# A decoder layer on one core: the half tiles of the output product in another order

## What is computed

```python
mix = gates[:, :, 0] * y_gla + gates[:, :, 1] * y_dsa
out = mix @ w_out[l]
x = x + gate_m * rmsnorm(out, g_post_mix[l])
h = rmsnorm(x, g_pre_ffn[l]) * (1.0 + scale_f) + shift_f
y = hier_moe(h, w_router_g[l], b_router_g[l], w_router_e[l], b_router_e[l], w_e_gate[l], w_e_up[l], w_e_down[l])
x = x + gate_f * rmsnorm(y, g_post_ffn[l])
```

## Time and profile before

| | |
|---|---|
| median of 3 runs | 761.08 us (760.99 to 763.07) |
| the profiled execution | 760.1 us, span of its records 758.3 us |
| TensorE busy | 684.6 us (90%) |
| VectorE busy | 410.4 us (54%) |
| ScalarE busy | 290.1 us (38%) |
| transfers | 179.27 MB, 236 GB/s over the span |

### The profile page before, as it was taken

How to read it: one execution, slowest core, us unless ns; L and a number is a source line. 1 busy time by engine, 2 the same in 40 slices (tenths; PEclk the granted TensorE clock), 3 DMA queues, 4 the chain that set the end, 5 groups by cost and what they waited for, 6 DMA issues and landing times.

```text
span 758.3 us, 9653 instructions
## 1 busy us (share of the span) xinstructions
PE 684.6 (90%) x3423; PEld 434.7 (57%) x3423; DVE 410.4 (54%) x867; ACT 290.1 (38%) x528; POOL 122.4 (16%) x156
## 2 busy tenths in 40 slices
PE   1899989998999989899999999989899978888785
PEld 0347757666777767778888888853333323333222
DVE  2376956998888886654523835645341211121127
ACT  5141435464486568643214233342121211121214
POOL 3056672320001011010000000040122111111100
PEclk9999989999999999999999999999989999999998
DMA  8989660411303030113334193999999999999973
GB/s 331 404 291 389 240 253 1 121 42 70 112 0 112 1 112 1 50 62 111 111 128 165 44 372 124 368 381 420 420 419 418 419 420 419 420 420 411 413 321 139
DMA packets 50319, 179.27 MB, mean 236 GB/s; under 512 B 9641, under 2 KB 13844, under 8 KB 36446
## 3 DMA queue, kind: packets, MB, share of 16 engines
q1 hardware_dynamic: 44502, 166.78, 56.2%
q0 software_dynamic: 4752, 8.18, 3.0%
q10 hardware_dynamic: 1016, 3.68, 1.3%
HBM read 174.13 MB, written 12.59 MB: 246 GB/s over the span
## 4 chain that ended last, share of the span: by engine, by line
PE 43%; DVE 22%; issue 7%; DMA 6%; SPq 5%; ACT 5%; DVEq 0%; POOL 0%; ACTq 0%; POOLq 0%
PE psA L498 8%; PE psA L500 7%; PE psA L499 7%; PE psS L916 6%; PE psA L945 5%; SPq L1130 4%; PE psG L916 4%; DVE mk_mem L1916 4%; DVE m L1915 3%; DMA arena<-in_w_e_up_dram 2%; DVE arena_r L1864 2%; DMA y_dram<-sig_mem,tables 2%; DVE mk_mem L1955 1%; DVE qs_mem L1935 1%; DVE qs_mem L2083 1%
## 5 line engine op out<-in xcount | busy, mean ns | idle before, releaser
L498 PE MATMUL psA<-arena_r 128*128 128x512 f32 x320 | 130.1, 406 | 0.0
L499 PE MATMUL psA<-arena_r 128*128 128x512 f32 x320 | 125.9, 393 | 0.0
L500 PE MATMUL psA<-arena_r 128*128 128x512 f32 x320 | 125.8, 393 | 0.0
L1864 DVE TENSOR_TENSOR arena_r<-arena,arena_r 128x1024 fp32r<-128x1024 f32 (+1 forms) x37 | 61.5, 1687 | 31.6 <-ACT arena_r L1377 30.5
L498 PEld LDWEIGHTS psA<-arena_r 128*128 128x128 f32 x320 | 60.9, 190 | 20.0 <-issue 8.1
L916 PE MATMUL psS<-arena,kv 128*64 128x512 f32 x224 | 59.9, 616 | 11.0 <-issue 9.3
L500 PEld LDWEIGHTS psA<-arena_r 128*128 128x128 f32 x320 | 60.8, 190 | 13.4
L499 PEld LDWEIGHTS psA<-arena_r 128*128 128x128 f32 x320 | 61.0, 191 | 12.1 <-issue 0.2
L916 PE MATMUL psG<-arena,kv 128*64 128x512 f32 x208 | 60.1, 630 | 6.3 <-issue 6.3
L1377 ACT CAST arena_r<-arena 128x1024 fp32r<-128x1024 f32 (+1 forms) x34 | 49.9, 1499 | 15.7 <-DMA arena<-in_w_in_dram 9.8
L2389 DVE TENSOR_TENSOR sig_mem<-sig_mem,psS 128x256 f32<-128x256 f32 x8 | 4.9, 611 | 77.0 <-ACT sig_mem L1710 77.0
(11 more groups left out here) (464 smaller groups left out, 1329.9 us busy)
## 6 DMA issues: line engine op xcount, KB each, us to landing
arena<-in_w_e_gate_dram SPq DMA_DIRECT2D x24, 1024.0 KB, 16.7
arena<-in_w_e_up_dram SPq DMA_DIRECT2D x24, 1024.0 KB, 19.7
arena<-in_w_in_dram SPq DMA_DIRECT2D x10, 2048.0 KB, 8.1
arena<-in_w_e_down_dram SPq DMA_DIRECT2D x12, 1024.0 KB, 19.2
qs_mem<-in_w_e_down_dram SPq DMA_DIRECT2D x10, 1024.0 KB, 23.4
arena<-in_w_ada_dram SPq DMA_DIRECT2D x4, 2048.0 KB, 16.6
qT<-in_w_ada_dram SPq DMA_DIRECT2D x6, 1024.0 KB, 5.0
gvs<-in_w_ada_dram SPq DMA_DIRECT2D x5, 1024.0 KB, 5.5
```

The source lines that it names most:

```text
L498: nc.tensor.matmul(acc, lhs[0], rhs[0], start=start, stop=False)
L499: nc.tensor.matmul(acc, lhs[0], rhs[1], start=False, stop=False)
L500: return nc.tensor.matmul(acc, lhs[1], rhs[0], start=False, stop=stop)
L1864: V.tensor_tensor(lo[:, part], src[:, part], hi[:, part], ALU.subtract).then_inc(lo_ready, 4 if q is None else 1)
```

## The change

The half tiles come in the order (0,0) (0,1) (1,0) **(2,0) (3,0) (1,1)** (2,1) (3,1). The work that hangs on tile 1 moves with (1,1): its turn goes into (2,1), its router into (3,1), its ranks behind router 2, its routing on VectorE behind `residual(2)`, its position behind `root_x1(2)`, its part of the first pair behind `residual(3)`, and its row store on ScalarE behind `out_root(2)`. The number and shapes of all instructions stay as they were.

```diff
-        out_order = [(0, 0), (0, 1), (1, 0), (1, 1), (2, 0), (3, 0), (2, 1), (3, 1)]
+        out_order = [(0, 0), (0, 1), (1, 0), (2, 0), (3, 0), (1, 1), (2, 1), (3, 1)]
...
             out_half(1, 0, turn=0)
-            out_half(1, 1, logits=0)
+            out_half(2, 0, logits=0)
+            out_half(3, 0)
             ranks(0)
-            out_half(2, 0, turn=1)
-            out_half(3, 0, logits=1)
+            out_half(1, 1)
+            out_half(2, 1, turn=1)
+            out_half(3, 1, turn=2, logits=1)
+            router(2)
             ranks(1)
-            out_half(2, 1)
-            out_half(3, 1, turn=2)
-            router(2)
             slots(0)
-            slots(1)
             first_rows(0, (0,))
             x1_turn(3, ("S0", "A0"))
             router(3)
+            slots(1)
             ranks(2)
...
             store_rows(0)
+            out_squares(2, 0)
+            out_squares(3, 0)
             out_squares(1, 1)
             out_root(1)
             x1_part(1)
-            out_squares(2, 0)
-            store_rows(1)
-            out_squares(3, 0)
             out_squares(2, 1)
             out_root(2)
+            store_rows(1)
             x1_part(2)
...
             out_scaled(1, 0)
+            out_scaled(2, 0)
             route(0)
+            out_scaled(3, 0)
+            position(0)
+            first_member(0)
             out_scaled(1, 1)
             residual(1)
-            position(0)
             turned(1)
             root_x1(1)
-            out_scaled(2, 0)
-            route(1)
-            out_scaled(3, 0)
-            position(1)
-            for tt in range(2):
-                first_member(tt)
-                first_slots(tt)
+            first_slots(0)
             out_scaled(2, 1)
             residual(2)
+            route(1)
             turned(2)
             root_x1(2)
+            position(1)
             out_scaled(3, 1)
             residual(3)
+            first_member(1)
+            first_slots(1)
             route(2)
```

## The result

| | before | changed |
|---|---|---|
| median of 4 runs, us | 761.04 (760.67 to 763.07) | 765.15 (764.33 to 766.25) |
| the profiled execution, its span, us | 760.1, 758.3 | 764.33, 762.5 |

The ratio is 1.0053, with a 95% interval of [1.0034, 1.0073]: slower, by 4.1 us. The forecast was 764.0.

The account below looks back on a forecast made before the run. The end was taken to hang on SyncE's weight-queue release, set by when VectorE begins route(2). +1.9 (wait) and +1.05 (moved work) gave +3.0 us: 763.1 profiled, 764.0 against the median; range 762.1, with some tenths, to 766.2.

Parts of the forecast that it names:

- the one number that decides: When VectorE begins route(2), now 490.06; the release of SyncE's weight queue and the first expert pair follow it; forecast +3.0 us.
- The loads' head start: SyncE's second-pair loads start 8.3 us earlier, near 466.4, but the queue then runs dry; costed at nothing.
- TensorE up to the end of (3,1): Same TensorE work in another order, ending 0.2 us earlier, with turns finding x1 ready; costed at nothing.
- the thin cover of `route(1)`: VectorE's route(1) and turned(2) end at 486.2, router 2 needs them at 486.24; cost nothing or a tenth.
- The wait of position(1): On VectorE, position(1) waits for ranks(1) behind router 2, so out_scaled(3,1) starts at 489.3 against 487.44: +1.9 us.
- The rival in which only the moved work counts: ranks(1) is there when VectorE reaches position(1), so no wait; +1.05 and up to 0.7 more, 762.1 to 762.8; chance 0.18.
- first_member(1) and first_slots(1): On VectorE they now stand between residual(3) and route(2), all on the path: +1.05 us.
- The clock, "so I add nothing": TensorE stops about 1.8 us ahead of the turn of tile 3; clock assumed to stay at 1.00, nothing added.
- the other end: If TensorE's clock falls to half at that stop, a further +2.8 us or so.
- The rival "the clock falls": TensorE's clock falls at the stop, or router 2 slips: +3.0 + 2.8, time 766.9; chance 0.10.
- The four loads: Sign that the forecast is right: SyncE issues the second pair's four loads near 466.4, now at 474.71.
- the wait ahead of line 2252: Sign that the forecast is right: VectorE idle there for tile 1 until ranks(1) releases it near 488.4.

Follow-up runs that it names:

- e1: The changed kernel with ranks(1) ahead of router 2 on TensorE; 762.75 us, ratio 1.0023.
- e2: The changed kernel with the second half of first_rows(0) and slots(1) moved ahead of the turn of tile 3 on TensorE; 763.34 us, ratio 1.0019.
- e5: The kernel before with only first_member(1) and first_slots(1) moved between residual(3) and route(2); 761.48 us, ratio 1.0004.
- e6: The kernel before with the third pair's second half of gate and up loads (2 MB) issued ahead of the wait for tile 3's rows; 761.81 us, ratio 0.9999.
- e9: The changed kernel with tile 1's position, first_member and first_slots behind route(2) on VectorE, and ranks(2) ahead of slots(1) on TensorE; 761.49 us, ratio 1.0004.
- e10: As e6 against the kernel before, but only one of the two 1 MB loads ahead of the wait; 762.91 us, ratio 1.0025.
- e11: As e7 against the kernel before, but only one of the two 1 MB loads ahead of the wait; 762.58 us, ratio 1.0020.
- e3: The changed kernel with SyncE waiting for (2,1) instead of (3,0) before the second pair's loads; 765.81 us, ratio 1.0049.
- e7: The kernel before with e6's earlier loads and router 1 inside (2,1) instead of (3,0); 761.06 us, ratio 0.9992.

## Why the prediction was right, and where it was off

*What bounds the kernel.* Held in part. Where the later places keep up, the end moves by as much as the release (e1 +1.7 and +1.6, e2 +3.0 and +2.9, e5 +1.0 and +1.0). But the release is not the one number that decides: the queue can run dry behind it, at the fourth pair's load (the change, 0.87 in 514 to 517) or at the fifth's (e6). In e6, e9, e10 and e11 the release moves by 0.0 to 0.4 and the fifth pair's load by 1.7 to 3.6.

*The loads' head start, costed at nothing.* Held, by e3 and by e9, as far as these can tell.

*TensorE up to the end of (3,1), and route(1), costed at nothing.* Held: TensorE has no stop from 464 to router 2, so the thin cover of `route(1)` was enough. That router 2 also began within 0.1 us of the forecast (486.40, 486.3) is partly luck, since the executions differ by up to 2.9 us there.

*The wait of position(1), +1.9.* Held: +1.96 at `out_scaled(3,1)`. (The terms written for it add up to 488.25, not 488.35; a tenth of the sum has no row.) e1 splits it into 0.66 of work that has no gap to hide in and 1.3 of waiting. The rival in which only the moved work counts became e1: its condition, `ranks(1)` there in time, was met by moving it ahead of router 2, and it gave the 1.7 us at the upper end of its price (762.8).

*first_member(1) and first_slots(1), +1.05.* Held: 492.01 to 493.06 in the change, and by themselves in e5.

*The clock, "so I add nothing".* This is the term that was mis-sized. The stop came as forecast, 1.89 us, and the clock did fall. I had put the stop beside the one of 1.5 us that left the clock at 1.00 and not the one of 3.5 us. The rule of the Trainium skill that was weighed there (TensorE: Matmul & The Clock Gate, section What's actually happening), half clock unless recent activity has released it, was the better guide in this place; the trace agrees with it, with 0.50 in 493 to 499. By the traces its price came out smaller than the +2.8 of the other end, 1.3: the release moves by only 0.4 through it, and the rest is the second dry place in 514 to 517. The rival "the clock falls", 766.9, was right in its mechanism and 1.8 too high. The measured 765.15 lies between the two cases: 764.0 + 1.3 = 765.3. By the timed runs the parts are others, 1.4 without the clock and 2.6 for it. Then +3.0 was too much, the clock's nothing too little, and the nearness of 764.0 to 765.15 would be luck in part.

*What should show it.* The four loads, the wait ahead of line 2252, `residual(3)`, `route(2)` came where they were said to come, and the dry stretch began some 1.5 us later (about 495 instead of 493); "the rest of the program later by the same 3 us" was wrong by the clock's share.

What stays open: the cost of the clock's fall to better than 1.3 to 2.6 us, and why the ends of single traces lie over the timed runs. No kernel was run that has the change's VectorE order and no stop of TensorE at all.

## What to carry to other kernels

When an order is changed, look for the first place in each engine's list where a piece of moved work or a moved wait stands ahead of the step that releases a queue; in this kernel a wait and a piece of work of 1 to 2 us there delayed the release by what they last, and a head start on the other side of that release bought nothing that the runs could show. Ask next what the delay stops: a stop of TensorE of a microsecond or two may also be paid for in its clock, and later work put into it (e2) kept the clock up here. Before an idle microsecond of a queue is filled, look for a short transfer on the path just behind it, and for the next place where the queue waits for a product: here all four tries moved the dry place and none gained.

## What was not expected of the hardware

The length of a stop of TensorE does not tell by itself whether its granted clock falls behind it. Here a stop of 1.49 us (before, ahead of 510.35) and two of 0.86 and 0.74 (e2) left it at 1.00, while one of 0.74 (e5) was followed by 0.50 in 493 to 496, 0.43 and 0.52 (e9) by 0.65, and 1.78 (e7) by 0.63. Where it fell, it stayed low for between some 3 us (e5) and some 10 (the change). Values between 0.50 and 1.00 are windows that hold stretches of both levels.

The store of half a megabyte by SyncE took 3.1 us from issue to landing behind an empty queue and 7.8 behind two loads of 1 MB that had been issued more than 10 us ahead of it (487.4 and 487.9 against 498.56 in e6).
